# A streaming encoder's opening with the value rows first, and its new latents joined by tokens

## The reference

```
h = RMSNorm(x);  P = h @ w_in      # pooling, window q/k/v, latent q (384), latent kv (256), rotary key (32), gates
A: multi-scale trailing means - token, per-group linear map
B: sliding-window attention (8 heads, 2 kv heads), QK-norm, position bias, sinks
C: c_kv = RMSNorm(kv_lat); kv = [cached latents, c_kv] @ w_kvup -> keys (8 x 64, + rotary 32, QK-norm), values (8 x 64)
   q = RMSNorm(q_lat) @ w_qup, QK-norm; chunk-causal attention over all keys
x += (sum_i sigmoid(gate_i) * (branch_i @ w_branch_i)) @ w_out
x += (silu(h2 @ w_gate) * (h2 @ w_up)) @ w_down,  h2 = RMSNorm(x)
```

## Time and profile before

| | |
|---|---|
| median of 3 runs | 1046.33 us (1045.97 to 1047.3) |
| the profiled execution | 1047.23 us, of which its span is 1045.3 us |
| busy over the span | PE 1038.8, PEld 1005.6, DVE 641.6, ACT 506.8, POOL 314.3 us |
| chain that ended last | PE 97%, DVE 2% |
| PE idle | 6.5 us: 1.26 before the first matmul, the last 2.7 after its end, the rest in the first 51 us |

### The profile page before, as it was taken

One profiled execution on the slowest core, in us unless ns is written; L12 is line 12 of the kernel. 1 busy time (PEld: TensorE's weight loads), 2 busy tenths in 40 slices (PEclk: granted clock), 3 DMA queues, 4 the chain that ended last, 5 costly groups with the idle time before them and its releaser, 6 DMA issues.

```text
span 1045.3 us, 20059 instructions
## 1 busy us (share of the span) xinstructions
PE 1038.8 (99%) x7586; PEld 1005.6 (96%) x7586; DVE 641.6 (61%) x1079; ACT 506.8 (48%) x930; POOL 314.3 (30%) x277
## 2 busy tenths in 40 slices
PE   8999999999999999999999999999999999999998
PEld 6899999999999999999998999999999999999998
DVE  6888764445766666543567886554557565565443
ACT  6557755444554444434355585554445444433341
POOL 3365566541221111100133755656312211111000
PEclk9999999999999999999999999999999999999999
DMA  7455533244535544454514544333344354444441
GB/s 243 118 157 124 185 103 120 90 133 142 161 120 164 159 146 155 142 180 145 178 45 137 149 145 135 96 119 122 120 154 152 124 177 141 154 147 146 156 145 67
DMA packets 48707, 146.29 MB, mean 140 GB/s; under 512 B 8800, under 2 KB 14400, under 8 KB 48640
## 3 DMA queue, kind: packets, MB, share of 16 engines
q1 hardware_dynamic: 42416, 143.05, 44.3%
q10 hardware_dynamic: 6224, 2.30, 0.9%
HBM read 142.11 MB, written 3.22 MB: 139 GB/s over the span
## 4 chain that ended last, share of the span: by engine, by line
PE 97%; DVE 2%; DMA 0%; ACT 0%; issue 0%; SPq 0%; ACTq 0%
PE psum L566 29%; PE psum L567 28%; PE psum L568 28%; PE psum L739 1%; PE psum L778 1%; PE psum L761 1%; PE psum L721 1%; PE psum L722 1%; PE psum L726 1%; PE psum L769 1%; PE psum L698 1%; PE psum L811 1%; PE psum L994 0%; PE psum L866 0%; PE psum L693 0%; PE psum L694 0%
## 5 line engine op out<-in xcount | busy, mean ns | idle before, releaser
L566 PE MATMUL psum<-AH,WH 128*128 128x320 f32 x1328 | 414.4, 312 | 0.2
L568 PE MATMUL psum<-AH,WL 128*128 128x320 f32 x1328 | 410.3, 309 | 0.0
L567 PE MATMUL psum<-AL,WH 128*128 128x320 f32 x1328 | 410.2, 309 | 0.0
L566 PEld LDWEIGHTS psum<-AH,WH 128*128 128x128 f32 x1328 | 249.3, 188 | 7.3 <-issue 5.5
L567 PEld LDWEIGHTS psum<-AL,WH 128*128 128x128 f32 x1328 | 249.4, 188 | 0.2
L568 PEld LDWEIGHTS psum<-AH,WL 128*128 128x128 f32 x1328 | 249.3, 188 | 0.0
L1077 ACT CAST WH<-raw 128x1024 fp32r<-128x1024 f32 x166 | 172.7, 1046 | 129.2 <-PE psum L568 127.7
L1515 DVE TENSOR_TENSOR WL<-raw,WH 128x1024 fp32r<-128x1024 f32 x103 | 127.6, 1240 | 114.0 <-ACT WH L1077 113.6
L1978 POOL TENSOR_TENSOR WL<-raw,WH 128x1024 fp32r<-128x1024 f32 x60 | 147.6, 2478 | 114.7 <-ACT WH L1077 95.5
L1709 DVE TENSOR_TENSOR WL<-raw,WH 128x1024 fp32r<-128x1024 f32 x88 | 107.5, 1222 | 49.5 <-ACT WH L1250 48.2
L1983 POOL TENSOR_TENSOR fab<-fa,fb 128x320 f32<-128x320 f32 x44 | 38.6, 878 | 264.6 <-DVE fb L1714 264.6
(11 more groups left out here) (284 smaller groups left out, 1580.1 us busy)
## 6 DMA issues: line engine op xcount, KB each, us to landing
raw<-w_all SPq DMA_DIRECT2D x264, 512.0 KB, 3.5
y_out<-X SPq DMA_DIRECT2D x8, 160.0 KB, 2.7
X<-x_in SPq DMA_DIRECT2D x2, 320.0 KB, 5.7
X<-x_in SPq DMA_DIRECT2D x1, 640.0 KB, 7.4
lat_out<-ckv ACTq DMA_DIRECT2D x2, 320.0 KB, 2.9
scratch<-brel SPq DMA_DIRECT2D x8, 63.8 KB, 4.3
ckv<-lat_in SPq DMA_DIRECT2D x1, 384.0 KB, 5.5
bias<-scratch SPq DMA_DIRECT2D x8, 48.0 KB, 4.5
```

The lines of the kernel that those rows point to most:

```text
L566: mm(out, WH[:, slot, c0:c0 + cols], high, start=first, stop=False)
L567: mm(out, WH[:, slot, c0:c0 + cols], low, start=False, stop=False)
L568: return mm(out, WL[:, slot, c0:c0 + cols], high, start=False, stop=last)
```

## The change

In the opening of layer 0 the value rows of block 0 come before its key rows. SP's first two transfers are the units U_KVV and U_KVK; the first cached latents and the rotary cache are issued by ACT, the gains by SP, and the remaining cached latents are loaded in two parts. The casts and subtractions of both units are halved, each half with its own semaphore, and the first latents' high part is made by DVE. The casts of the first unit's activation chunks (`norm_chunk`) and their low parts stand at other places between the key blocks. In the join the new latents are divided by tokens (0 to 127, 128 to 319) instead of by their two feature halves, the sum over the partitions in layer 0 comes behind the dense tile T_QL+1 and not in its middle, and the evictions of the three query tiles stand at other places.

```diff
--- before.py
+++ after.py
+LATENTS = (((0, 128), (128, 256), (256, PAST)), ((0, 128), (128, PAST)))
...
     @block.sync
...
-        sp.dma_start(ckv[:, :, T:T + 128], lat[:, :, 0:128]).then_inc(s.cache_lat[0], 16)
-        sp.dma_start(raw[:, 0, :], w_all[stored(0)]).then_inc(raw_ready[0], 16)
-        sp.dma_start(raw[:, 1, :], w_all[stored(1)]).then_inc(raw_ready[1], 16)
+        sp.dma_start(raw[:, U_KVV, :], w_all[stored(U_KVV)]).then_inc(raw_ready[U_KVV], 16)
+        sp.dma_start(raw[:, U_KVK, :], w_all[stored(U_KVK)]).then_inc(raw_ready[U_KVK], 16)
+        sp.dma_start(ckv[:, :, T + 128:T + 256], lat[:, :, 128:256]).then_inc(s.cache_lat[1], 16)
         sp.dma_start(cst[:, K_ID:K_ID + 128], cst_in[:, K_ID:K_ID + 128]).then_inc(s.id_in, 16)
-        sp.dma_start(krT[64:96, T:NKEY], kr_in[0:1].rearrange("a p n -> (a p) n")).then_inc(s.cache_kr, 16)
-        sp.dma_start(ckv[:, :, T + 128:NKEY], lat[:, :, 128:PAST]).then_inc(s.cache_lat[1], 16)
         sp.dma_start(par[:, 0:DEPTH * NPAR], par_in).then_inc(s.par_in, 16)
+        gain_pairs = par_in.rearrange("p (l c) -> p l c", c=NPAR)[:, :, C_GQ:C_GQ + 2]
+        for row, at_row in ((96, 80), (112, 64)):
+            sp.dma_start(gains[row:row + 16], gain_pairs[at_row:at_row + 16]).then_inc(s.gains_in, 16)
+        sp.dma_start(ckv[:, :, T + 256:NKEY], lat[:, :, 256:PAST]).then_inc(s.cache_lat[2], 16)
...
         def key_rows(l, kb):
...
+            if kb == 2:
+                pe.wait_ge(s.ckv_ready, CKV0[l] + len(LATENTS[l]))
...
             for c in range(2):
+                if l == kb == 0:
+                    pe.wait_ge(s.high_ready if c else s.first_high, 2 if c else 3)
                 mm(out, ckvH[:, c, keys], wh[:, c], start=c == 0, stop=False)
...
         def value_rows(l, kb):
...
             for c in range(2):
+                if l == kb == 0:
+                    pe.wait_ge(s.first_high, 1 + c)
                 mm(out, ckvH[:, c, keys], WKH[:, U_KVV, c * 512:c * 512 + 512], start=c == 0, stop=False)
...
             for kb in range(CACHED):
-                key_rows(l, kb)
-                value_rows(l, kb)
+                if l == kb == 0:
+                    value_rows(l, kb)
+                    key_rows(l, kb)
+                else:
+                    key_rows(l, kb)
+                    value_rows(l, kb)
...
             if l > 0:
                 latent_sum(l)
-            dense(l, U_QL + 1, T_QL + 1, between=(lambda: latent_sum(l)) if l == 0 else None)
+            dense(l, U_QL + 1, T_QL + 1)
+            if l == 0:
+                latent_sum(l)
             turn_rope(l, 1)
             dense(l, U_QL + 2, T_QL + 2)
...
+        act.dma_start(ckv[:, :, T:T + 128], lat_in[0:1].rearrange("a p c n -> (a p) c n")[:, :, 0:128]) \
+            .then_inc(s.cache_lat[0], 16)
+        act.dma_start(krT[64:96, T:NKEY], kr_in[0:1].rearrange("a p n -> (a p) n")).then_inc(s.cache_kr, 16)
         act.wait_ge(s.warm_zero, 1)
         A(small[:, 31:32], ssum[:, 0:1], ACT.Sqrt)
-        cached_high(0, 0)
...
-        high(0, U_KVK)
-        high(0, U_KVV)
+        act.wait_ge(raw_ready[U_KVV], 16)
+        for c in range(2):
+            half = slice(512 * c, 512 * c + 512)
+            nc.scalar.copy(WKH[:, U_KVV, half], raw[:, U_KVV, half]).then_inc(s.first_high, 1)
+        act.wait_ge(raw_ready[U_KVK], 16)
...
+        cached_high(0, 1)
...
             high(l, U_POOL)
+            act.wait_ge(s.ckv_first, l + 1)
+            nc.scalar.copy(ckvH[:, :, 0:128], ckv[:, :, 0:128]).then_inc(s.ckv_high, 1)
             act.wait_ge(s.stat_applied, l * NNORM + N_KV + 1)
-            nc.scalar.copy(ckvH[:, 0, 0:T], ckv[:, 0, 0:T]).then_inc(s.ckv_high, 1)
-            act.wait_ge(s.ckv_second, l + 1)
-            nc.scalar.copy(ckvH[:, 1, 0:T], ckv[:, 1, 0:T]).then_inc(s.ckv_high, 1)
+            nc.scalar.copy(ckvH[:, :, 128:T], ckv[:, :, 128:T]).then_inc(s.ckv_high, 1)
             rope_rows(l, 1)
...
+        dve.wait_ge(s.cache_lat[0], 16)
+        v.tensor_copy(ckvH[:, :, T:T + 128], ckv[:, :, T:T + 128]).then_inc(s.first_lat, 1)
         cached_low(0, 0)
-        low(0, U_KVK)
-        low(0, U_KVV)
+        for c in range(2):
+            half = slice(512 * c, 512 * c + 512)
+            dve.wait_ge(s.first_high, 1 + c)
+            TT(WKL[:, U_KVV, half], raw[:, U_KVV, half], WKH[:, U_KVV, half].bitcast(F32), ALU.subtract) \
+                .then_inc(s.first_low, 1)
...
-            r = recip(l, N_KV, 128, T)
-            STT(ckv[:, 0, 0:T], kvr[:, 0, :], col(C_MKV, l), r, ALU.mult, ALU.mult).then_inc(s.stat_applied, 1)
-            STT(ckv[:, 1, 0:T], kvr[:, 1, :], col(C_MKV + 1, l), r, ALU.mult, ALU.mult).then_inc(s.ckv_second, 1)
             scaled(l, T_QL, qlr[:, 0, :])
-            for c in range(2):
-                dve.wait_ge(s.ckv_high, 2 * l + c + 1)
-                ins = TT(ckvL[:, c, 0:T], ckv[:, c, 0:T], ckvH[:, c, 0:T].bitcast(F32), ALU.subtract)
-            ins.then_inc(s.ckv_ready, 1)
-            scaled(l, T_QL + 1, qlr[:, 1, :])
+            dve.wait_ge(s.std_ready, l * NSTAT + N_KV + 2)
+            for n, keys in enumerate((slice(0, 128), slice(128, T))):
+                r = stdk[:, N_KV % 2, keys]
+                link(l, v.reciprocal(r, r))
+                if n == 1:
+                    scaled(l, T_QL + 2, qlr[:, 2, :])
+                for c in range(2):
+                    ins = STT(ckv[:, c, keys], kvr[:, c, keys], col(C_MKV + c, l), r, ALU.mult, ALU.mult)
+                ins.then_inc(s.stat_applied if n else s.ckv_first, 1)
+                if n == 0:
+                    scaled(l, T_QL + 1, qlr[:, 1, :])
+                dve.wait_ge(s.ckv_high, 2 * l + n + 1)
+                TT(ckvL[:, :, keys], ckv[:, :, keys], ckvH[:, :, keys].bitcast(F32), ALU.subtract).then_inc(s.ckv_ready, 1)
             dve.wait_ge(s.both_high, l + 1)
...
             low(l, U_POOL)
-            scaled(l, T_QL + 2, qlr[:, 2, :])
```

More of the change, by code:

```diff
@@ L111 @@
 HALF = 64
+LATENTS = (((0, 128), (128, 256), (256, PAST)), ((0, 128), (128, PAST)))
+CKV0 = (0, 5)
 def fresh(kb):
@@ L153, in __init__ @@
         self.rstd_ready = sem("rstd_ready")
-        self.cache_lat = [sem(f"cache_lat{i}") for i in range(2)]
+        self.cache_lat = [sem(f"cache_lat{i}") for i in range(3)]
+        self.first_high = sem("first_high")
+        self.first_lat = sem("first_lat")
+        self.first_low = sem("first_low")
         self.cache_kr = sem("cache_kr")
@@ L1095, in cached_high @@
         def cached_high(l, part):
-            keys = (slice(T, T + 128), slice(T + 128, NKEY))[part]
+            keys = slice(*(T + c for c in LATENTS[l][part]))
             act.wait_ge(s.cache_lat[part], 16 * l + 16)
@@ L1291, in _ @@
                         norm_chunk(l, 0, 2, square=False)
+                    else:
                         norm_chunk(l, 0, 3, square=False)
-                elif kb < 2:
-                    norm_chunk(l, 0, 4 + 2 * kb, high=False)
-                    norm_chunk(l, 0, 5 + 2 * kb, high=False)
-                elif kb == 2:
-                    high(l, U_KV + 1)
+                        key_columns(l, kb - 1)
+                        act.wait_ge(s.x_in[2], 16)
+                        norm_chunk(l, 0, 4, square=False)
+                        norm_chunk(l, 0, 5, square=False)
+                        key_root(l, kb)
+                        norm_chunk(l, 0, 6, square=False)
+                        norm_chunk(l, 0, 7, square=False)
+                else:
+                    key_square(l, kb)
+                    value_copy(l, kb)
+                    if kb == 0:
+                        rope_rows(l, 0)
+                    key_root(l, kb)
+                    if kb > 0:
+                        key_columns(l, kb - 1)
+                    if kb < 2:
+                        norm_chunk(l, 0, 4 + 2 * kb, high=False)
+                        norm_chunk(l, 0, 5 + 2 * kb, high=False)
+                    elif kb == 2:
+                        high(l, U_KV + 1)
             if l == 0:
-                act.wait_ge(s.x_in[2], 16)
-                for k in range(4, KC):
-                    norm_chunk(l, 0, k, square=False)
                 for k in range(KC):
@@ L1517, in cached_low @@
         def cached_low(l, part):
-            keys = (slice(T, T + 128), slice(T + 128, NKEY))[part]
-            dve.wait_ge(s.ckv_cache_high, 2 * l + part + 1)
+            keys = slice(*(T + c for c in LATENTS[l][part]))
+            if l == part == 0:
+                dve.wait_ge(s.first_lat, 1)
+            else:
+                dve.wait_ge(s.ckv_cache_high, 2 * l + part + l)
             TT(ckvL[:, :, keys], ckv[:, :, keys], ckvH[:, :, keys].bitcast(F32), ALU.subtract).then_inc(s.ckv_ready, 1)
@@ L1567, in key_scale @@
             if l == 0 and kb == 2:
-                dve.wait_ge(s.split_ready, U_KV + 1)
-                low(l, U_KV + 1)
+                norm_low(l, 0, 0)
+                norm_low(l, 0, 1)
             if kb == KB - 1:
@@ L1740, in _ @@
```

(8 more changed lines are left out.)

79 lines of the change are left out of this document (50 added, 29 removed).

## The result

| | before | the change |
|---|---|---|
| median, 6 runs each | 1047.02 us (1045.97 to 1047.42) | 1052.8 us (1050.31 to 1053.02) |
| the profiled execution | 1047.23 us, span 1045.3 | 1052.86 us, span 1051.1 |
| ratio to before | | 1.0054, 95% interval 1.0044 to 1.0064 |

The change made the kernel slower by about half a per cent. The forecast was 1048.1 us, with 1044.2 to 1050.6 as its range: the measured time lies above it, and above the rival of two falls of the clock, 1049.8.

A forecast was written before the change was run, and what follows sets the result against it. The kernel was taken as bound by TensorE (PE busy 1038.8 of 1045.3 us). Opening -2.3, layer 0's join +0.5 and layer 1's +1.9 give +0.1; one clock fall makes it +1.8 on the median 1046.33: 1048.1 us, range 1044.2 to 1050.6.

The forecast's parts named there:

- the rival of two falls of the clock: Block 4's turning, both layers: the clock falls behind both waits of PE, 1049.8 us; chance 0.17.
- The opening: Layer 0's start: block 0 turned at 12.65 instead of 15.00, -2.3 us, bounds -3.0 and -1.1.
- should be there by then: Opening: the first latents, issued by ACT and cast by idle DVE, are there by the first value matmul, about 5.85.
- The waits in the join: Block 4's turning: PE waits for POOL, 2.0 to 2.1 us in layer 0 and 1.6 in layer 1.
- The 0.4 us that I allowed on top: Layer 1's join: POOL's addition for block 4, queued behind its own subtraction, may add up to 0.4 us.
- one of my bounds: Layer 0's join: upper bound +1.0 us, if krm's step on DVE delays it by 0.4 too.
- layer 0's join: Join of layer 0: -1.6 us of old pauses against a new wait of 2.1, net +0.5, bounds -1.6 and +1.0.
- layer 1's: Join of layer 1: a new wait of PE at block 4's turning, +1.9 us, bounds 0 and +2.4.
- The clock: Behind the two waits at block 4's turning: one fall to half clock, costing 1.7 us, is likeliest; chance 0.33.
- The rival in which nothing falls: Block 4's turning, both layers: the clock holds behind both waits, 1046.4 us; chance 0.28.

The follow-up runs named there:

- the second profile of the same kernel: The full change timed again, unchanged, with its own profile, against the kernel before: 1051.73 us, ratio 1.0045.
- the two kernels with the opening alone: The change with the join put back as before: 1045.34 us; the same with layer 0's eviction of T_QL+2 ahead of DVE's subtraction of U_POOL: 1045.47 us.
- the join alone: The kernel before with the new join in both layers and the old opening: 1051.44 us, ratio 1.0051.
- the later eviction: The changed kernel with the eviction of T_QL+2 moved behind the products of the second part of the latents: 1047.56 us, ratio 1.0014.
- the filled wait: The changed kernel with nine more matmuls of 512 columns on PE ahead of block 4's turning in each layer: 1049.36 us, ratio 1.0027.
- the 33 executions of those kernels: The changed kernel with one move each: eviction of T_QL+2 later (1047.56 us), krm's mean steps first (1048.84), POOL's subtraction later (1048.21).

## Why the prediction failed

**The opening** came as worked out in its number: -2.31 us at the first turning against -2.3, block 1's keys at 9.56 against 9.7, the first value matmul at 5.99 against 5.85. The reason for the last was another than I gave: the weights were there 0.9 us sooner than I had put, and the latents, which "should be there by then", set the start. What failed is the step from the first turning to the end, where I carried the whole term. Of it 0.8 us was given back before the join began: block 1's turning waited 0.3 (16.40 to 16.70), and the first statistics' sum came only 1.5 us ahead. In the second profile of the same kernel the lead there was 2.8 us, so this part is not fixed by the order; I have no experiment on it. And the 15.00 that I subtracted from held a pause of 1.4 us and a fall of the clock that another execution of the same opening did not have (13.76), and that few executions of before have (4 of 72); yet I put the difference on the median. By the medians the opening is worth 1.1 us, by the ratio 0.8.

**The waits in the join** were foreseen, with their places: the second cast of the latents, behind it the unit's cast, the square, POOL's addition. In layer 1 every step up to the square came within 0.1 us of the forecast, counted from the latent sum: the cast at 9.45 (I had put 565.37 - 555.99 = 9.38), the square at 11.80 (11.71). But from the square to POOL's end it was 4.14 us, where I had put 3.34. That is the term that was mis-sized, by 0.8 us in each layer. I had taken it as it stood in layer 1 of before, where POOL's subtraction had ended 0.5 us before the DVE step on `krm`. With the new order that subtraction stands across the step, and the step ends with it. The 0.4 us that I allowed on top was for POOL's queue in layer 1, and in layer 0 for `krm` as one of my bounds. With POOL's subtraction out of the way the wait was 1.0 us less in each layer, and block 4 of layer 1 was turned 15.04 us behind the latent sum, where the forecast has POOL's end at 15.05.

In layer 0 the wait of 2.38 us lies near the 2.0 to 2.1 by luck. POOL's end came 12.8 us behind the latent sum instead of 11.7, but PE too came to the turning later than I had put, 10.5 instead of 9.7 us behind the sum. Part of that is a wait for which I had no term: block 5's keys start 0.71 us behind the step before (48.32 to 49.03), where 0.46 is the usual distance, because the low part of the second latents ends only at 48.98. In the sum, layer 0's join cost 1.4 instead of 0.5, layer 1's 2.5 instead of 1.9.

The Trainium skill, page "SBUF — State Buffer", section "SBUF: two separate sides", says of the pair of ports that VectorE and GpSimd share that it is "an exclusive lock, not a bandwidth split", held by whichever instruction starts first, and counts VectorE instructions in a two-port mode among those that need it. The traces agree in thirteen places: each time the step ran beside POOL's subtraction (layer 0 of before and of the two kernels with the opening alone, both layers of both profiles of the change, of the join alone, of the later eviction and of the filled wait) it ended 0.02 to 0.03 us behind it. It took 0.17 us where POOL was idle, while the reduction of the same columns just ahead of it took its usual 0.24 us beside POOL. That this step runs in such a mode is not shown by any row. I had not drawn on this page; it would have pointed to the missing 0.8 us.

**The clock** was the step that failed outright: one fall was put at 0.33 and two at 0.17. Both came in both profiles of the change and in seven of its eleven executions, and at least one in every one of them. The filler shows that the pause is the cause. The length of the pause alone does not decide it: behind 1.44 us it fell in the opening, behind 2.35 it held once and fell once in one execution, behind 1.87, 1.78 and 1.39 it held in the profiles, and fell in two of the 33 executions of those kernels. The rival in which nothing falls is out with the two falls, and so, for this kernel, is the rule of the Trainium skill, page "TensorE: Matmul & The Clock Gate", section "Why this matters for your kernels", that only longer pauses need to be avoided. What sets it between two pauses of one length stays open.

**The sum, term by term**, by the two first profiles: -1.5 (forecast -2.3), +1.4 (+0.5), +2.5 (+1.9), two falls +3.4 (one, +1.7): 5.8 instead of 1.8. Of the 4.0 us missed, 1.7 is the second fall, 0.8 the opening's lead, 1.5 the join. So the second fall alone would have brought the time to the rival's 1049.8; the joins and the opening carried it past that.

## What to carry to other kernels

A pause of the engine that bounds the kernel can cost its length and, here, 1.7 us of clock besides: price it as both, and, where it can't be removed, harmless work in it is cheaper than the pause. When an order is changed, list for every engine what now runs *beside* each step, not only what it waits for: a step of three columns took 1.7 us because of its neighbour. One profile of before may itself hold an unlucky pause, and then a gain worked out against it must not be put on the median: compare its mean clock with that of the other executions first.

## What the runs showed of the hardware

- VectorE's `TENSOR_SCALAR` on 128x3 in SBUF took 0.17 us alone and 0.58 to 1.72 us beside GpSimd's 2.4 us subtraction, ending 0.02 to 0.03 us behind it in all thirteen cases. Without the trace's end times it looks like a slow instruction.
- TensorE's granted clock held at 1.00 behind a pause of 2.35 us and fell to 0.55 behind another of 2.35 us in the same execution (1.2 GHz against 2.4 at 1.00); with the same pause filled to 0.35 us it held in both layers. By the mean clocks, kernels with two pauses of 2.33 to 2.38 us had 23 falls in 16 executions, kernels whose longest pause was 1.39 to 1.87 us had two in 33.
- The same opening set the first matmul of data at 6.42 in one execution and 7.04 in another, since one transfer landed 0.6 us later; the first turning of keys then differed by 1.24 us.
